# Projecting the values of two strided groups with the keys in partitions, in a decoder layer with dilated attention

## Chip, cores and metric

One Trainium2 chip, one core. The kernel is one program launched once. The metric is the device time of that launch in microseconds (us), the median of several executions.

## What is computed

One decoder layer for 512 tokens of width 1024, in float32: adaLN modulation, a mixture of three causal dilated window attentions, a gated convolutional FFN and a last RMSNorm. The part that matters here is the attention:

```python
DSW_PATTERNS = ((128, 1), (512, 4), (2048, 16))     # window, dilation of the three groups
qkv = (h @ w_in).reshape(B, S, 3, DSW_GROUPS, DSW_HEADS, DSW_HEAD_DIM)
for g, (window, dilation) in enumerate(DSW_PATTERNS):
    o, lse = dilated_window_attention(qkv[:, :, 0, g], qkv[:, :, 1, g], qkv[:, :, 2, g], window, dilation)
...
weights = jax.nn.softmax(jnp.stack(lses, axis=0), axis=0)
o = jnp.sum(weights[..., None] * jnp.stack(outs, axis=0), axis=0)
return o.reshape(B, S, D_MODEL).astype(h.dtype) @ w_out
```

In groups 1 and 2 (dilation 4 and 16) a query attends only to keys whose position has the same remainder, so their tokens are ordered by the remainder modulo 4.

## The kernel before

**Strips.** The 16 heads are worked in 8 pairs. A pair n has nine weight strips of 1024 x 128: values of groups 0, 1, 2 (s = 0, 1, 2), then query and key of each group (s = 3 to 8). A strip's raw weights come by DMA (SP's queue) into one of three buffers `raw`. ScalarE (ACT) writes their high part `wh` (`split_qkv`, profile line L1059), VectorE (DVE) writes the low part `wl` = raw - wh (L1348), each into a slot of a ring of four, of which three are in use after the first pair. TensorE (PE) multiplies a strip in 24 matmuls: for each of the eight tiles of the model width wl x hh, wh x hh, wh x hl (L742, L743, L744). The weights are the stationary operand and the 512 tokens are moving, so the product has the head dimension in partitions and tokens in columns. ACT copies it out of the bank (L1115).

**Values are turned.** The product of probabilities and values (`weigh_values`) wants values with the keys in partitions. So a value strip goes to `v_t`, and `turn_values` transposes it on PE, four blocks of 128 tokens (L784), for groups 1 and 2 each block taking every fourth token. DVE (groups 0 and 2, L1403) or ACT (group 1, L1118) then copies it into `v_n`.

**The order.** `bodies` runs body(n) for n = 0 to 8: pair n is projected while pair n-1 is attended. All engines walk the same 18 half strips h (s = h // 2) and hang their other work on them by hand-written tables. In bodies 1 to 7:

- PE at h: half strip h, then by table a turn of values (`TURN_V_AT`, h = 3, 5, 7), scores (`SCORE_AT`: d = 0, 1 at h = 0, d = 2, 3 at h = 4), transposed probabilities and their product with the values (h = 12 to 16).
- ACT at h: splitting the high part of a strip (`split_at`: at even h, strip h // 2 + 2), at odd h copying out strip s, and exponentials of score part d (`MASK_AT`: d = 0 to 3 at h = 0, 1, 4, 5; L1130).
- DVE at h: the low part of the same strip, a step of the adaLN sum `acc` (L1453, eight to a body; step t = 4, at h = 5, waits for the second half of `ada_raw` to land), copying turned values, and at `MASK_AT` masking the scores and taking their maximum (L1418, ending with `nmax`, L1424), which the exponentials wait for.
- SP: `load_strips` issues strip s once the high and low part of strip s - 3 are made. The second half of `ada_raw` (L529) is issued behind strip 5, once the first four steps of `acc` are done.

PE waits for the low part of a strip at its first half (`l_ready`). ACT waits for the raw weights and for the strip that used the slot before (`strip_done`). Every engine runs its own list in order, so what stands behind a waiting instruction waits too.

Of the kernel before, what the change touches and what calls it, by code (L numbers as in the profile page):

```python
# [26 lines left out]
T = 512  # L27
D = 1024
KT = D // P
# [3 lines left out]
GROUPS = 3  # L33
# [11 lines left out]
RING = 3  # L45
# [35 lines left out]
def decoder_layer(nc, x, c, w_ada, b_ada, norm_mix, norm_ffn, attn_w_in, attn_w_out,  # L81
# [11 lines left out]
    with ctx:  # L93
# [154 lines left out]

        SCORE_AT = {0: (0, 1), 4: (2, 3)}
        MASK_AT = {0: 0, 1: 1, 4: 2, 5: 3}  # L250
        TURN_V_AT = {3: 0, 5: 1, 7: 2}
        ADA_READ_AT = {0: 0, 1: 1, 2: 2, 3: 3, 5: 4, 6: 5, 7: 6, 8: 7}
        ADA_AT = 10
        TURN_P_AT = {12: (0, 1), 14: (2, 3)}
# [33 lines left out]
            return banks[s] if is_first(n) and s in (2, 3) else proj[(par + s) % 2]  # L288

        def qkv_slot(n, s):  # L290
            return RING if is_first(n) and s == RING else s % RING

        def score_bank(d, hd):

# [5 lines left out]

        def split_at(n, h):

            if h % 2:
                return None
            if is_first(n) and h < 8:
                return h // 2 + FIRST if h < 4 else None
            return h // 2 + 2

        def out_slot(o):

# [336 lines left out]
        def _(pe):  # L647
# [91 lines left out]
            def half_strip(bank, slot, half, xh, xl):  # L739
# [4 lines left out]
                    last = nc.tensor.matmul(bank[:], wh[:, slot, t], xl[:, t], start=False, stop=(t == KT - 1))  # L744
                return last

            def make_scores(n, par, d):

                if d == 0:
                    pe.wait_ge(strip_taken, STRIPS * n)  # L750
                if d == 1:
                    pe.wait_ge(ada_taken, n)
                if d >= 2:
                    pe.wait_ge(masked, 4 * (n - 1) + d - 1)
                side, tiles = d // 2, (2 * (d % 2), 2 * (d % 2) + 1)
                for b in tiles:
                    at = HALF * (b % 2)
                    if side == 0:
                        lo = P * max(b - 1, 0)
                        for hd in range(2):  # L760
                            e = slice(E * hd, E * (hd + 1))
                            last = nc.tensor.matmul(score_bank(d, hd)[:, at + (P if b == 0 else 0):at + HALF],  # L762
                                                    q_t[e, par, 0, P * b:P * (b + 1)],
                                                    k_t[e, par, 0, lo:P * (b + 1)], start=True, stop=True)
                    else:
                        for g in (1, 2):
                            for hd in range(2):
                                e = slice(E * hd, E * (hd + 1))
                                last = nc.tensor.matmul(score_bank(d, hd)[:, at + P * (g - 1):at + P * g],  # L769
                                                        q_t[e, par, g, P * b:P * (b + 1)],  # L770
                                                        k_t[e, par, g, P * b:P * (b + 1)], start=True, stop=True)
                last.then_inc(scored, 1)

            def turn_values(n, par, g):
                k, use = g % 2, g // 2
                pe.wait_ge(strip_taken, STRIPS * n + g + 1)
                if use:
                    pe.wait_ge(v_taken[0], 2 * n + 1)
                elif not is_first(n):
                    pe.wait_ge(o_summed, n)  # L780
                src = v_t[:, (par + g) % 2]
                for b in range(NT):
                    keys = src[:, P * b:P * (b + 1)] if g == 0 else src[:, b:T:4]
                    last = nc.tensor.transpose(o_acc[k][:, P * b:P * (b + 1)], keys, ident[:])  # L784
                last.then_inc(v_turned[k], 1)
# [23 lines left out]
            def weigh_values(n, par, j, project):  # L809

                for hd in range(2):
                    pe.wait_ge(p_taken[hd], 4 * (n - 1) + j + 1)
                if j == 0:
                    pe.wait_ge(o_summed, n)
                    if project:
                        pe.wait_ge(v_taken[0], 2 * n + 2)
                        pe.wait_ge(v_taken[1], n + 1)
                side = j // 2
                blocks = p_blocks(j)
                for i, (b, part) in enumerate(blocks):  # L820
                    first = i == 0 or blocks[i - 1][0] != b
                    final = i == len(blocks) - 1 or blocks[i + 1][0] != b
                    for hd in range(2):
                        e = slice(E * hd, E * (hd + 1))
                        if side == 0:
                            values = v_n[:, par, 0, b - 1 + part, e]
                        else:
                            values = v_n[:, par, 1 + part, b, e]
                        last = nc.tensor.matmul(o_acc[side][e, P * b:P * (b + 1)], values,  # L829
                                                p_t[:, (2 * j + hd) % PT_RING, P * i:P * (i + 1)],  # L830
                                                start=first, stop=final)
                last.then_inc(pv_done, 1)
# [37 lines left out]
            def body(n, par, project, attend):  # L870
                filled = 0
                for h in range(2 * FIRST if is_first(n) else 0, HALVES):
                    s = h // 2
                    if project:
                        g = STRIPS * n + s
                        if h % 2 == 0:
                            pe.wait_ge(l_ready, g + 1)
                            pe.wait_ge(strip_taken, s - RING if is_first(n) and s < FIRST + 2 else g - 1)
                        last = half_strip(qkv_bank(n, par, s), qkv_slot(n, s), h % 2, hh, hl)
                        if h % 2 == 1:  # L880
                            last.then_inc(strip_done, 1)
                        turn_v_at = TURN_V_FIRST if is_first(n) else TURN_V_AT
                        if h in turn_v_at:
                            turn_values(n, par, turn_v_at[h])
                        if h == (ADA_FIRST if is_first(n) else ADA_AT):
                            sum_ada(n)
                    if attend:
                        if h in SCORE_AT:
                            for d in SCORE_AT[h]:
                                make_scores(n, 1 - par, d)  # L890
                        for j in PV_AT.get(h, ()):
                            weigh_values(n, 1 - par, j, project)
                        for j in (TURN_P_AT if project else TURN_P_LAST).get(h, ()):
                            for u in (2 * j, 2 * j + 1):
                                turn_probs(n, u, project)
                    if attend and not project and h in FILL_AT:
                        begin_out(fill_steps[filled:filled + FILL_AT[h]])
                        filled += FILL_AT[h]
# [128 lines left out]
        def _(act):  # L1027
# [31 lines left out]
                nc.scalar.activation(dst, src, ACT.Copy).then_inc(done, 1)  # L1059

            def split_qkv(n, s):
                g = STRIPS * n + s
                free = None if isinstance(g, int) and g <= RING else (strip_done, g - RING + 1)
                slot = qkv_slot(n, s)
                split_h(raw_in[s % RING], 16 * (GROUPS * n + s // RING + 1), raw[:, s % RING], wh[:, slot],
                        free, h_ready)

            def copy_rows(c):

# [31 lines left out]
            def body(n, par, project, attend):  # L1101
                for h in range(HALVES):
                    s = h // 2
                    if project:
                        if split_at(n, h) is not None:
                            split_qkv(n, split_at(n, h))
                        if h % 2 == 1:
                            act.wait_ge(strip_done, STRIPS * n + s + 1)
                            kind, g = strip_of(s)

                            if is_first(n) and s == 2:
                                act.wait_ge(v_turned[0], 1)
                            dst = {"v": v_t[:, (par + g) % 2], "q": q_t[:, par, g], "k": k_t[:, par, g]}[kind]
                            src, dst = in_order(g, kind, qkv_bank(n, par, s)[:], dst)
                            nc.scalar.activation(dst, src, ACT.Copy).then_inc(strip_taken, 1)  # L1115
                        if (TURN_V_FIRST if is_first(n) else TURN_V_AT).get(h) == 1:
                            act.wait_ge(v_turned[1], n + 1)
                            nc.scalar.activation(v_n[:, par, 1].rearrange("p b e -> p (b e)"), o_acc[1][:], ACT.Copy  # L1118
                                                 ).then_inc(v_taken[1], 1)
# [174 lines left out]
        def _(dve):  # L1294
# [104 lines left out]
                start_low(c)  # L1399

            def take_values(n, g, dst):
                dve.wait_ge(v_turned[0], 2 * n + g // 2 + 1)
                nc.vector.tensor_copy(dst, o_acc[0][:]).then_inc(v_taken[0], 1)  # L1403

            def take_probs(n, j, project):
# [391 lines left out]
```

## Time and profile before

| | |
|---|---|
| median of 3 runs | 971.48 us (971.14 to 971.8) |
| the profiled execution | 971.24 us |
| its span, first to last instruction | 969.2 us |
| PE busy | 943.0 us, 97% of the span |
| DVE busy | 598.9 us, 62% |
| ACT busy | 447.9 us, 46% |
| TensorE clock granted, mean | 0.996 of full |

The profile is of one execution. Times in it are counted from the start of the span. A matmul's shown duration holds its latency too and overlaps the next one's, so what a matmul costs in a stream is the distance between starts.

### The profile page before, as it was taken

The numbers are of one execution on the slowest core, as the hardware profiler recorded it, in microseconds if no ns is written. First come the engines' busy times: TensorE is split into PE (matmuls) and PEld (weight loads), VectorE is DVE, ScalarE is ACT, GpSimd is POOL, SyncE is SP. The second block draws the span as 40 slices with busy tenths as digits, with TensorE's granted clock in tenths as the row PEclk, the third lists the DMA queues.
The fourth block names the chain that finished last, engine by engine and source line by source line (L and its number), as shares of the span: only waits on it lengthen the run. The fifth ranks groups of instructions, "written<-read, shape, count | busy, mean of one in ns | idle before, by whom it ended". The sixth has DMA issues, their size and how long they took to land.

```text
span 969.2 us, 16362 instructions
## 1 busy us (share of the span) xinstructions
PE 943.0 (97%) x5828; PEld 800.2 (83%) x5828; DVE 598.9 (62%) x1304; ACT 447.9 (46%) x804; POOL 19.9 (2%) x39
## 2 busy tenths in 40 slices
PE   7999999999999999999999899999999999999996
PEld 6687887888888888888787788889999999888884
DVE  3445655725737457366473757899999999633325
ACT  7244434436344354363443455655555556523222
POOL 2000000000000000000000001400000000000000
PEclk9999999999999999999999999999999999999999
DMA  9765342433424323344143022433343343532302
GB/s 310 237 199 149 113 127 65 122 118 108 132 62 130 110 91 102 108 124 136 44 131 108 23 58 74 109 88 87 92 125 87 87 124 93 156 105 87 108 1 87
DMA packets 151538, 107.01 MB, mean 110 GB/s; under 512 B 3510, under 2 KB 138830, under 8 KB 151502
## 3 DMA queue, kind: packets, MB, share of 16 engines
q1 hardware_dynamic: 151296, 106.45, 36.6%
q8 instruction: 23, 0.38, 0.2%
q14 instruction: 13, 0.11, 0.0%
q10 hardware_dynamic: 206, 0.08, 0.0%
HBM read 104.42 MB, written 2.10 MB: 110 GB/s over the span
## 4 chain that ended last, share of the span: by engine, by line
PE 73%; DVE 14%; issue 5%; ACT 5%; POOL 1%; DVEq 1%; ACTq 0%; POOLq 0%
PE bank L742 14%; PE bank L744 13%; PE bank L743 13%; DVE wl L1348 4%; PE bank L1002 4%; PE bank L1001 4%; PE bank L1003 4%; PE bank L829 3%; PE bank L805 3%; DVE gate_in L1619 3%; ACT wh L1059 2%; PE bank L769 1%; DVE sums L1653 1%; DVE sums L1650 1%; PE bank L762 1%
## 5 line engine op out<-in xcount | busy, mean ns | idle before, releaser
L1348 DVE TENSOR_TENSOR wl<-raw,wh 128x1024 fp32r<-128x1024 f32 (+1 forms) x127 | 150.1, 1183 | 175.5 <-ACT wh L1059 174.9
L742 PE MATMUL bank<-hh,wl 128*128 128x512 f32 x544 | 221.3, 407 | 0.0
L744 PE MATMUL bank<-hl,wh 128*128 128x512 f32 x544 | 215.4, 396 | 0.0
L743 PE MATMUL bank<-hh,wh 128*128 128x512 f32 x544 | 215.2, 396 | 0.0
L1059 ACT ACTIVATE wh<-raw 128x1024 fp32r<-128x1024 f32 (+1 forms) x127 | 130.1, 1026 | 63.6 <-PE bank L1003 52.2
L742 PEld LDWEIGHTS bank<-hh,wl 128*128 128x128 f32 x544 | 102.7, 189 | 25.8 <-issue 3.5
L744 PEld LDWEIGHTS bank<-hl,wh 128*128 128x128 f32 x544 | 102.4, 188 | 24.4
L743 PEld LDWEIGHTS bank<-hh,wh 128*128 128x128 f32 x544 | 102.6, 189 | 21.5
L952 PE MATMUL bank<-th,wl 128*128 128x256 f32 x304 | 87.4, 287 | 5.2 <-DVE up_late L1687 4.3
L1130 ACT ACTIVATE probs<-probs,nmax 128x256 f32<-128x256 f32 (+1 forms) x128 | 61.9, 485 | 65.8 <-DVE nmax L1424 65.8
L954 PE MATMUL bank<-th,wh 128*128 128x256 f32 x304 | 85.5, 281 | 0.0
L955 PE MATMUL bank<-tl,wh 128*128 128x256 f32 x304 | 85.5, 281 | 0.0
L952 PEld LDWEIGHTS bank<-th,wl 128*128 128x128 f32 x304 | 57.3, 189 | 8.8 <-DVE up_late L1687 7.6
L952 PE MATMUL bank<-fh,wl 128*128 128x256 f32 x228 | 64.2, 282 | 0.2 <-DVE wl L1348 0.2
L954 PE MATMUL bank<-fh,wh 128*128 128x256 f32 x228 | 64.1, 281 | 0.0
L955 PE MATMUL bank<-fl,wh 128*128 128x256 f32 x228 | 64.1, 281 | 0.0
L1001 PE MATMUL bank<-act_h,wl 128*128 128x512 f32 x160 | 63.4, 396 | 0.0
L1002 PE MATMUL bank<-act_h,wh 128*128 128x512 f32 x160 | 63.4, 396 | 0.0
L1003 PE MATMUL bank<-act_l,wh 128*128 128x512 f32 x160 | 63.4, 396 | 0.0
L954 PEld LDWEIGHTS bank<-th,wh 128*128 128x128 f32 x304 | 57.4, 189 | 0.0
L955 PEld LDWEIGHTS bank<-tl,wh 128*128 128x128 f32 x304 | 57.4, 189 | 0.0
L1059 ACT ACTIVATE wh<-sums 128x1024 fp32r<-128x1024 f32 x38 | 40.5, 1065 | 33.8 <-DVE sums L1653 24.0
(217 smaller groups left out, 1604.2 us busy)
## 6 DMA issues: line engine op xcount, KB each, us to landing
raw<-in_attn_w_in SPq DMA_DIRECT2D x72, 512.0 KB, 3.8
raw<-in_ffn_w_up SPq DMA_DIRECT2D x34, 512.0 KB, 4.0
ada_raw<-in_w_ada SPq DMA_DIRECT2D x16, 1024.0 KB, 5.9
raw<-in_ffn_w_down SPq DMA_DIRECT2D x17, 512.0 KB, 3.3
raw_up<-in_ffn_w_up SPq DMA_DIRECT2D x10, 512.0 KB, 5.1
ada<-in_w_ada SPq DMA_DIRECT2D x16, 256.0 KB, 6.8
raw<-in_attn_w_out SPq DMA_DIRECT2D x8, 512.0 KB, 4.3
raw_up<-in_ffn_w_down SPq DMA_DIRECT2D x5, 512.0 KB, 3.4
```

Source lines behind the costliest of these rows:

```text
L742: nc.tensor.matmul(bank[:], wl[:, slot, t], xh[:, t], start=(t == 0), stop=False)
L743: nc.tensor.matmul(bank[:], wh[:, slot, t], xh[:, t], start=False, stop=False)
L744: last = nc.tensor.matmul(bank[:], wh[:, slot, t], xl[:, t], start=False, stop=(t == KT - 1))
L952: nc.tensor.matmul(bank[:, 0:HALF], low, xh[:, t], start=(fresh and t == 0), stop=False, skip_group_check=True)
L954: nc.tensor.matmul(bank[:, 0:HALF], high, xh[:, t], start=False, stop=False, skip_group_check=True)
L955: last = nc.tensor.matmul(bank[:, 0:HALF], high, xl[:, t], start=False, stop=(final and t == HK - 1), skip_group_check=True)
L1001: nc.tensor.matmul(y[:], wl[:, u, o], act_h[:, u], start=start, stop=False)
L1002: nc.tensor.matmul(y[:], wh[:, u, o], act_h[:, u], start=False, stop=False)
L1003: last = nc.tensor.matmul(y[:], wh[:, u, o], act_l[:, u], start=False, stop=False)
L1059: nc.scalar.activation(dst, src, ACT.Copy).then_inc(done, 1)
L1130: last = nc.scalar.activation(tile, tile, ACT.Exp, bias=nmax[:, side, b, hd:hd + 1], scale=SCORE_SCALE, accum_out=stat[:, side, b, 1, hd:h ...
L1348: nc.vector.tensor_tensor(dst, src, high.bitcast(F32), ALU.subtract).then_inc(done, 1)
```

## The change

Groups 1 and 2 of the values are projected the other way round in bodies 1 to 7. In `key_block` the stationary operand is a block of 128 tokens, every fourth one (`hh[:, t, b:T:4]`), and the moving operand is 256 columns: the weights of group 1 and of group 2 side by side, from slots 1 and 3 of the ring (`wh[:, 1:4:2, t]`). Four such blocks take the place of strips 1 and 2, one at each of h = 2 to 5. Their product has the keys in partitions already and is copied straight into `v_n`. The first pair stays as it was.

Both strips' weights must be there at h = 2, and both slots stay occupied until h = 5 is done. So strip 2 goes to the fourth slot, and strip 4, which uses slot 1, is no longer split at h = 4 but at h = 6, with the wait for strip 2's product (`strip_done` of 9n + 3); strip 5 is split at h = 7 (before: h = 6). Group 0's turn of values is at h = 4 (before: 3); the turns of groups 1 and 2 and their two copies are gone.

```diff
-        TURN_V_AT = {3: 0, 5: 1, 7: 2}
+        TURN_V_AT = {4: 0}
+        KEYS_AT = {2: 0, 3: 1, 4: 2, 5: 3}
...
         def qkv_slot(n, s):
-            return RING if is_first(n) and s == RING else s % RING
+            return RING if s == (RING if is_first(n) else 2) else s % RING
...
         def split_at(n, h):
-            if h % 2:
+            if is_first(n) and h < 8:
+                return h // 2 + FIRST if h in (0, 2) else None
+            if not is_first(n) and h in (4, 6, 7):
+                return {4: None, 6: 4, 7: 5}[h]
+            return None if h % 2 else h // 2 + 2
+
+        def qkv_free(n, s):
+            g = STRIPS * n + s
+            if isinstance(g, int) and g <= RING:
                 return None
-            if is_first(n) and h < 8:
-                return h // 2 + FIRST if h < 4 else None
-            return h // 2 + 2
+            return strip_done, g - 1 if s == 4 and not is_first(n) else g - RING + 1
...
+            def key_block(n, par, b):
+                bank = qkv_bank(n, par, 1 + b // 2)
+                out = bank[:, HALF * (b % 2):HALF * (b % 2 + 1)]
+                for t in range(KT):
+                    keys = slice(b, T, 4)
+                    nc.tensor.matmul(out, hh[:, t, keys], wl[:, 1:4:2, t], start=(t == 0), stop=False)
+                    nc.tensor.matmul(out, hh[:, t, keys], wh[:, 1:4:2, t], start=False, stop=False)
+                    last = nc.tensor.matmul(out, hl[:, t, keys], wh[:, 1:4:2, t], start=False, stop=(t == KT - 1))
+                return last
...
                         if h % 2 == 0:
-                            pe.wait_ge(l_ready, g + 1)
+                            pe.wait_ge(l_ready, g + 2 if s == 1 else g + 1)
...
-                        last = half_strip(qkv_bank(n, par, s), qkv_slot(n, s), h % 2, hh, hl)
+                        if h in KEYS_AT:
+                            last = key_block(n, par, KEYS_AT[h])
+                        else:
+                            last = half_strip(qkv_bank(n, par, s), qkv_slot(n, s), h % 2, hh, hl)
...
+                            if s in (1, 2) and not is_first(n):
+                                src = qkv_bank(n, par, s)[:].rearrange("p (b g e) -> p g b e", b=2, g=2)
+                                dst = v_n[:, par, 1:3, 2 * (s - 1):2 * s]
```

## Rows read from the trace of the kernel before

**Rows 1.** The page: span, and TensorE's line of busy time.
```profile
span 969.2 us, 16362 instructions
PE 943.0 (97%) x5828; PEld 800.2 (83%) x5828; DVE 598.9 (62%) x1304; ACT 447.9 (46%) x804; POOL 19.9 (2%) x39
```
**Rows 2.** Busy time by stretch: bodies 1 and 6, of equal length.
```profile
core 0: us, PE busy (x) PEld busy (x) DVE busy (x) ACT busy (x) POOL busy (x), PEclk, DMA share, GB/s
90.72:154.21 63.49, 63.49 (x372) 51.67 (x372) 35.13 (x101) 27.07 (x58) 0.00 (x0) 1.00 0.36 109
...
408.18:471.67 63.49, 63.49 (x372) 51.68 (x372) 35.74 (x102) 28.00 (x59) 0.00 (x0) 1.00 0.36 108
```
**Rows 3.** Timeline, TensorE with 512 columns: start, duration, engine, line.
```profile
402.32 0.19 PEld L742 LDWEIGHTS bank<-hh,wl 128*128 128x128 f32 x1 [0.17 <-issue]
402.43 0.19 PEld L743 LDWEIGHTS bank<-hh,wh 128*128 128x128 f32 x1
...
403.12 0.39 PE L742 MATMUL bank<-hh,wl 128*128 128x512 f32 x1
...
407.31 0.40 PE L742 MATMUL bank<-hh,wl 128*128 128x512 f32 x1
```
**Rows 4.** Timeline, TensorE with 256 columns, in the FFN.
```profile
699.98 0.29 PE L952 MATMUL bank<-th,wl 128*128 128x256 f32 x1
...
705.66 0.28 PE L952 MATMUL bank<-fh,wl 128*128 128x256 f32 x1
```
**Rows 5.** Timeline around group 1's turn of values in body 6.
```profile
426.30 0.40 PE L744 MATMUL bank<-hl,wh 128*128 128x512 f32 x1
...
426.54 0.63 PE L784 MATMUL bank<-ident,v_t 128*128 128x128 f32 x4
...
427.24 0.40 PE L743 MATMUL bank<-hh,wh 128*128 128x512 f32 x1
```
**Rows 6.** Weight loads: every fourth token (min/median/max ns), and contiguous ones (mean ns).
```profile
L784 PEld LDWEIGHTS bank<-ident,v_t x4: 197/207/212, 426.3 to 426.8; 128*128 128x128 f32 x4
...
L742 PEld LDWEIGHTS bank<-hh,wl 128*128 128x128 f32 x544 | 102.7, 189 | 25.8 <-issue 3.5
...
L792 PEld LDWEIGHTS bank<-ident,acc 128*128 128x128 f32 x32 | 4.0, 141 | 1.1
```
**Rows 7.** Timeline of body 6: strip 2's low part, then the steps to strip 5's.
```profile
409.40 1.23 DVE L1348 TENSOR_TENSOR wl<-raw,wh 128x1024 fp32r<-128x1024 f32 x1
...
420.55 0.37 SPq L529 DMA_DIRECT2D ada_raw<-in_w_ada  x1
...
426.70 0.75 DVE L1453 SCALAR_TENSOR_TENSOR acc<-ada_raw,cond,acc 128x512 f32<-128x512 f32 x1 [2.02 <-DMA ada_raw<-in_w_ada]
...
428.86 0.17 DVE L1424 TENSOR_SCALAR nmax<-stat 128x4 f32<-128x4 f32 x1
...
431.06 1.04 ACT L1059 ACTIVATE wh<-raw 128x1024 fp32r<-128x1024 f32 x1
...
432.13 1.23 DVE L1348 TENSOR_TENSOR wl<-raw,wh 128x1024 fp32r<-128x1024 f32 x1 [3.10 <-ACT wh L1059]
...
433.01 0.48 PE L742 MATMUL bank<-hh,wl 128*128 128x512 f32 x1
```
**Rows 8.** Timelines: strip 5's low part in bodies 1, 3 and 7; a table load.
```profile
114.84 1.23 DVE L1348 TENSOR_TENSOR wl<-raw,wh 128x1024 fp32r<-128x1024 f32 x1 [3.10 <-ACT wh L1059]
...
217.96 1.28 ACT L1059 ACT_TABLE_LOAD   x1
...
242.70 1.23 DVE L1348 TENSOR_TENSOR wl<-raw,wh 128x1024 fp32r<-128x1024 f32 x1 [3.10 <-ACT wh L1059]
...
495.25 1.22 DVE L1348 TENSOR_TENSOR wl<-raw,wh 128x1024 fp32r<-128x1024 f32 x1 [3.10 <-ACT wh L1059]
```
**Rows 9.** Transfers: time to landing of all 16 of `ada_raw`; raw strips issued behind one.
```profile
DMA to landing us min/median/max: 5.4/5.9/7.1
...
421.23 28.10 SPq L522 DMA_DIRECT2D raw<-in_attn_w_in  x6
```

More of the change, by code:

```diff
@@ L777, in turn_values @@
                 if use:
-                    pe.wait_ge(v_taken[0], 2 * n + 1)
+                    pe.wait_ge(v_taken[0], 1)
                 elif not is_first(n):
@@ L815, in weigh_values @@
                     if project:
-                        pe.wait_ge(v_taken[0], 2 * n + 2)
-                        pe.wait_ge(v_taken[1], n + 1)
+                        pe.wait_ge(v_taken[0], n + 2)
+                        pe.wait_ge(v_taken[1], 1)
                 side = j // 2
@@ L1061, in split_qkv @@
             def split_qkv(n, s):
[L1062 to L1066, printed above, removed]
+                split_h(raw_in[s % RING], 16 * (GROUPS * n + s // RING + 1), raw[:, s % RING], wh[:, qkv_slot(n, s)],
+                        qkv_free(n, s), h_ready)
             def copy_rows(c):
@@ L1112, in body @@
                                 act.wait_ge(v_turned[0], 1)
-                            dst = {"v": v_t[:, (par + g) % 2], "q": q_t[:, par, g], "k": k_t[:, par, g]}[kind]
-                            src, dst = in_order(g, kind, qkv_bank(n, par, s)[:], dst)
+                            if s in (1, 2) and not is_first(n):
+                                src = qkv_bank(n, par, s)[:].rearrange("p (b g e) -> p g b e", b=2, g=2)
+                                dst = v_n[:, par, 1:3, 2 * (s - 1):2 * s]
+                            else:
+                                dst = {"v": v_t[:, (par + g) % 2], "q": q_t[:, par, g], "k": k_t[:, par, g]}[kind]
+                                src, dst = in_order(g, kind, qkv_bank(n, par, s)[:], dst)
                             nc.scalar.activation(dst, src, ACT.Copy).then_inc(strip_taken, 1)
@@ L1401, in take_values @@
             def take_values(n, g, dst):
-                dve.wait_ge(v_turned[0], 2 * n + g // 2 + 1)
+                dve.wait_ge(v_turned[0], g // 2 + 1 if is_first(n) else n + 2)
                 nc.vector.tensor_copy(dst, o_acc[0][:]).then_inc(v_taken[0], 1)
```

## The prediction

> **What bounds the kernel now.** First the page: the span is 969.2 us and PE is busy 943.0 of it, 97%, against 62% for DVE and 46% for ACT [rows 1]. A share over the whole says little about one stage, so next the busy time by stretch: each of the full bodies takes 63.49 us, and PE is busy for all 63.49 of them, at the full granted clock (1.00, the 2.4 GHz level) [rows 2]. The reader is to see that no wait of PE is left in the projection loop. Whatever shortens PE's list there shortens the body, until another engine's chain is late. The change can act in seven bodies (1 to 7). I measure places in a body from the edges of those stretches (408.18 for body 6) and call that its phase.
>
> **PE's own work, per body.** Two value strips are 48 matmuls of 512 columns now. Eighteen of them lie between 403.12 and 407.31, so one costs 4.19 / 18 = 0.2328 us [rows 3], and 48 cost 11.17 us. The new blocks are 96 matmuls of 256 columns. The FFN has that form: 48 between 699.98 and 705.66, 5.68 / 48 = 0.1183 us each [rows 4]; 96 cost 11.36 us. That is +0.19 us, the same columns in twice as many instructions.
>
> Removed are two turns, those behind h = 5 and h = 7. Around the first, two matmul starts that in a stream lie 2 x 0.2328 = 0.466 us apart are 427.24 - 426.30 = 0.94 us apart [rows 5]: a turn costs 0.474 us, with its four transposes and the breaks at both ends. The second looks the same. Two give -0.95 us. Group 0's turn only moves from the end of h = 3 to that of h = 4 and costs PE the same; its copy on DVE falls ahead of the mask of d = 2, into time in which DVE waits for scores. The two copies out of the bank that vanish (one ACT, one DVE) gain nothing by themselves, as PE does not wait for either engine now [rows 2]. PE alone: -0.76 us a body, -5.3 us in seven.
>
> **The strided stationary operand.** No row has a float32r load of every fourth column. The nearest are the transposes of v_t, whose loads step by the same four elements: 207 ns against 141 ns for a contiguous transpose load, 66 ns more [rows 6]. A contiguous load of the matmul form shows 189 ns [rows 6], but the next one starts 0.11 us after it [rows 3], so it holds the weight path about 0.11 us and hides under a 0.118 us matmul, barely. From below: the load may hide altogether under the matmul (118 ns). From above: 66 ns are added in full to 110, 176 ns a matmul, 96 x 0.058 = +5.5 us a body. I take 118 to 125 ns, because four strided transposes take 0.63 us [rows 5], so with one latency of about 0.28 us at the end they start some 0.12 us apart, each with its strided load; the excess, at most 0.6 us a body, falls ahead of h = 6 and is swallowed by the wait below.
>
> The Trainium skill speaks against this operand: "SBUF — State Buffer", section "Door 1: The DMA port swizzle", says that SBUF reads run at full rate only with at least two hits in a 16-byte line, and four float32 elements are 16 bytes, so each read here touches a new line. The 207 against 141 ns [rows 6] agree that there is a price. By that rule the matmuls would be load-bound, which is the third case below; by the transposes' spacing they are not.
>
> **Waits that the new order makes.** At h = 2 PE now needs strip 2 as well. Its low part is done at 409.40 + 1.23 = 410.63, phase 2.5 [rows 7]; h = 2 begins near phase 4.4 (after the body's edge PE still has the first scores and one half strip of 12 x 0.2328 = 2.79 us). It is hidden with 2 us to spare.
>
> Strip 4 is the delicate one. It stands at h = 6 in the lists of ACT and DVE, which is behind the exponentials and the mask of d = 3. That is just where strip 5 stands today, so the trace of before shows when it will be ready. In body 6: the ada transfer is issued at 420.55; DVE waits 2.02 us for it and starts step t = 4 at 426.70; then the mask of d = 3, whose maximum comes at 428.86; four exponentials; the split at 431.06; the low part from 432.13 to 433.36, phase 25.18 [rows 7]. None of these steps waits for the slot (PE leaves h = 5 near 426.5) or for what the change takes away. Today strip 5 is needed only at h = 10, so nobody sees this chain. With the change PE wants strip 4 at h = 8.
>
> When does PE reach h = 8? Today at 433.01, phase 24.83 [rows 7]; without the two turns and with the blocks' +0.19 at phase 24.07. The ends of strip 5's low part in the seven bodies are at phases 25.35, 25.51, 26.23, 25.04, 26.50, 25.18 and 24.80 [rows 7, 8]. Bodies 3 and 5 are late because ACT loads a table for 1.28 us at their start [rows 8]. The mean is 25.52. With 0.1 us from semaphore to first matmul the wait is 25.52 + 0.1 - 24.07 = 1.55 us a body, 10.8 us in seven.
>
> One thing may shorten it. The ada transfer takes 5.4 to 7.1 us, median 5.9 [rows 9], and about 6.1 in the seven places that count. Behind it go the raw loads of strips 6 and 7 [rows 9]. Strip 7's buffer will be free only after the new, later split of strip 4, so one competitor of 512 KB is gone. Between no gain and 0.7 us (the fastest of the 16) I take 0.3: an estimate from these rows. The wait becomes 1.25 us a body, 8.7 us in seven.
>
> Behind the waiting matmul stands all of PE's list, and every later anchor moves with it, so nothing is given back. DVE has one more low part and one less copy between h = 6 and h = 8, some 0.5 us later against work at h = 12 and on, where PE also comes 0.5 us later: no second wait. Strips 5 to 8 are loaded and split with several us to spare.
>
> **Sum.** -5.3 + 8.7 = +3.4 us. The profiled execution took 971.24 us (span 969.2) and the median of the runs is 971.48, 0.24 away. I forecast 971.48 + 3.4, about **975 us**. Without the gain in the transfer it would be 977, with the full 0.7 about 972.
>
> **Rivals.**
>
> *Hidden after all (faster).* Strip 4 is ready in time because the ada transfer lands before about 425.5 in body 6 instead of 426.7 and correspondingly elsewhere. Then only PE's own -5.3 us is left: 966 us. For it: a competitor in the queue is removed, and it decides at 1.5 us earlier on average. Against it: no transfer of the 16 was faster than 5.4 us, 0.7 less than the mean here. A mixture, the wait gone in bodies 4, 6 and 7 and halved elsewhere, is a draw.
>
> *A draw.* The transfer gains 0.5 to 1.0 us, or a turn was worth more than 0.47: 970 to 973 us.
>
> *The strided weight load is the bound.* 176 ns a matmul gives -0.95 + 0.19 + 5.5 = +4.7 us a body, and the wait for strip 4 is then covered: +33 us, 1005 us. If a strided load took twice the 0.11 us, 0.22, it would be 96 x 0.102 = +9.8 us, +63 us, 1035. It decides from about 0.131 us a matmul: up to there the excess hides in the wait. For it: the 66 ns. Against it: the transposes' spacing.
>
> *The change does not do what it says* is not to be expected: instructions fall by eight transposes and rise by 48 matmuls a body whatever the time.
>
> **Chances.** The new wait with a loss of over 0.2%: 0.50. Draw, within 0.2% (1.9 us, about what a measurement of this kernel can tell from no change): 0.19. Faster: 0.20. Strided loads bound: 0.11, also slower. Slower in all 0.61. For the range I leave out the strided-load case and a little at each end: 967 to 982 us, where 982 is the 977 of no gain in the transfer plus 0.7 us a body for a slower restart or a chain that slips.
>
> **What the profile after would show.** The chain of waits in the loop: PE at L742 (h = 8) waiting for DVE's L1348, about 1.2 us, seven times, longest in bodies 3 and 5; bodies of about 64.0 us with PE busy some 62.7. The blocks' matmuls 118 to 125 ns apart, their loads above 189 ns. The ada transfer landing in 5.4 to 6.1 us. I am wrong if that wait is missing (transfer early), if the blocks' starts lie over 131 ns apart, or if a wait shows at h = 2 or at the transposes of h = 12.

## The result, and the profile after

The changed kernel takes 1045.43 us (median of 4 runs, 1044.4 to 1049.79), the kernel before 971.31 us beside it: a ratio of 1.0775 (95% interval 1.0741 to 1.0809), 74 us slower. I had forecast 975 us, in a range of 967 to 982. The direction was right, the size wrong by a factor of twenty, and the direction was right by another mechanism than the one I forecast: the case that I had given 11 in 100, the strided load as the bound, is what happened, and in its dearer form.

The page of the changed kernel, with the lines that answer to those of before [rows 1], the new matmul and its weight load, and the queue that fetches instructions:

```profile
span 1044.1 us, 16891 instructions
## 1 busy us (share of the span) xinstructions
PE 1014.1 (97%) x6108; PEld 886.0 (85%) x6108; DVE 595.5 (57%) x1297; ACT 444.5 (43%) x797; POOL 19.9 (2%) x39
...
q8 instruction: 42, 0.69, 0.3%
...
L761 PE MATMUL bank<-wl,hh 128*128 128x256 f32 x224 | 89.1, 398 | 0.0
...
L761 PEld LDWEIGHTS bank<-wl,hh 128*128 128x128 f32 x224 | 73.5, 328 | 1.2
```

PE is as busy as before, 97%. Its share says nothing about the loss; the mean of one load does: 328 ns, where a contiguous load of this form shows 189 [rows 6].

Busy time by stretch, bodies 1 to 3 (same columns as [rows 2]):

```profile
90.67:164.31 73.64, 73.64 (x412) 64.10 (x412) 34.55 (x100) 26.54 (x57) 0.00 (x0) 1.00 0.31 93
164.31:239.76 75.45, 73.89 (x412) 64.02 (x412) 35.93 (x102) 29.27 (x60) 0.00 (x0) 1.00 0.31 92
239.76:313.41 73.65, 73.65 (x413) 64.13 (x412) 34.54 (x100) 27.02 (x57) 0.00 (x0) 1.00 0.31 93
```

A body went from 63.49 us [rows 2] to 73.64, at the same full granted clock of 1.00. Two of the seven (the second here, and body 4) are 1.8 us longer still. The timeline of the changed kernel shows both causes. First the blocks, in body 2: the start of the block at h = 2 (168.86), two matmuls inside it that are 21 apart (170.84 and 175.74), and the last matmul of the block at h = 4 (185.31):

```profile
168.86 0.28 PE L761 MATMUL bank<-wl,hh 128*128 128x256 f32 x1
...
170.84 0.40 PE L761 MATMUL bank<-wl,hh 128*128 128x256 f32 x1
...
172.81 0.33 PEld L761 LDWEIGHTS bank<-wl,hh 128*128 128x128 f32 x1
...
175.74 0.40 PE L761 MATMUL bank<-wl,hh 128*128 128x256 f32 x1
...
185.31 0.40 PE L763 MATMUL bank<-wh,hl 128*128 128x256 f32 x1
...
234.75 0.40 PE L752 MATMUL bank<-hl,wh 128*128 128x512 f32 x1
...
236.71 0.50 PE L750 MATMUL bank<-hh,wl 128*128 128x512 f32 x1 [1.56 <-ACT k_t L1138]
```

4.90 / 21 = 0.2333 us a matmul, twice the 0.1183 of 256 columns in the FFN [rows 4]; over the three blocks in a row, 72 matmuls, 16.45 / 71 = 0.2317. The last two rows stand at the end of body 2 and the start of body 3, where the loop over two bodies jumps back. PE is idle for 1.56 us there. The view names ACT's copy as the releaser, but PE's wait at that point is for an older strip, long copied.

The sum closes with these. The blocks take 96 x 0.2317 = 22.24 us instead of 11.17, which is +11.07. A later kernel with contiguous blocks and no wait for a strip (below, new slots) has bodies of 62.59 us, 0.90 shorter than before, and its blocks take 96 x 0.117 = 11.2 us, 0.03 more than the strips had; so two turns are worth about 0.93 us. That gives +10.14 us a body (measured 10.15), 71.0 in seven; two jumps of 1.84 us add 3.7. Together 74.7 us, against 74.1 between the medians.

### The profile page after: what moved, and what is told of

It is laid out like the page before. It is cut to its first block, busy times and chain, and to the rows that moved or that the text cites. A ratio compares the mean times of both kernels' runs of the same rounds, so it can differ in the third digit from the quotient of the medians.

```text
span 1044.1 us, 16891 instructions
## 1 busy us (share of the span) xinstructions
PE 1014.1 (97%) x6108; PEld 886.0 (85%) x6108; DVE 595.5 (57%) x1297; ACT 444.5 (43%) x797; POOL 19.9 (2%) x39
## 4 chain that ended last, share of the span: by engine, by line
PE 73%; DVE 13%; issue 5%; ACT 5%; POOL 1%; DVEq 1%; DMA 1%; SPq 1%; ACTq 0%
PE bank L750 10%; PE bank L752 10%; PE bank L751 10%; PE bank L761 5%; PE bank L763 5%; PE bank L762 5%; DVE wl L1371 4%; PE bank L1023 4%; PE bank L1025 4%; PE bank L1024 4%; PE bank L848 3%; PE bank L824 3%; DVE gate_in L1642 2%; ACT wh L1081 2%; PE bank L788 1%
## 5 line engine op out<-in xcount | busy, mean ns | idle before, releaser
L750 PE MATMUL bank<-hh,wl 128*128 128x512 f32 x432 | 174.5, 404 | 3.2 <-ACT k_t L1138 3.2
L752 PE MATMUL bank<-hl,wh 128*128 128x512 f32 x432 | 170.9, 396 | 0.0
L751 PE MATMUL bank<-hh,wh 128*128 128x512 f32 x432 | 170.7, 395 | 0.0
L750 PEld LDWEIGHTS bank<-hh,wl 128*128 128x128 f32 x432 | 81.3, 188 | 24.9 <-ACT k_t L1138 4.0
L763 PE MATMUL bank<-wh,hl 128*128 128x256 f32 x224 | 89.1, 398 | 0.0
L761 PE MATMUL bank<-wl,hh 128*128 128x256 f32 x224 | 89.1, 398 | 0.0
L762 PE MATMUL bank<-wh,hh 128*128 128x256 f32 x224 | 89.0, 397 | 0.0
L761 PEld LDWEIGHTS bank<-wl,hh 128*128 128x128 f32 x224 | 73.5, 328 | 1.2
L763 PEld LDWEIGHTS bank<-wh,hl 128*128 128x128 f32 x224 | 73.8, 329 | 0.0
L762 PEld LDWEIGHTS bank<-wh,hh 128*128 128x128 f32 x224 | 73.6, 329 | 0.0
```

What stands on the lines that cost most here:

```text
L750: nc.tensor.matmul(bank[:], wl[:, slot, t], xh[:, t], start=(t == 0), stop=False)
L751: nc.tensor.matmul(bank[:], wh[:, slot, t], xh[:, t], start=False, stop=False)
L761: nc.tensor.matmul(out, hh[:, t, keys], wl[:, 1:4:2, t], start=(t == 0), stop=False)
L762: nc.tensor.matmul(out, hh[:, t, keys], wh[:, 1:4:2, t], start=False, stop=False)
L763: last = nc.tensor.matmul(out, hl[:, t, keys], wh[:, 1:4:2, t], start=False, stop=(t == KT - 1))
```

## Experiments

Each time is a median: of 10 executions for the contiguous, the ordered and the new-slots kernel and the control, 8 for every second token, 4 for the two other versions with TensorE's program written out, and 2 for the rest, whose effects are far above the scatter. Each ratio is to the kernel before, run beside it.

### The pace of the blocks: the step, or the form?

Contiguous tokens, the one edit in `key_block` (the blocks then project other tokens than they should):

```diff
-                    keys = slice(b, T, 4)
+                    keys = slice(P * b, P * (b + 1))
```

> The changed kernel with one edit: each block takes 128 tokens in a row as its stationary operand instead of every fourth one (so it projects other tokens than it should; every count, shape, wait and the moving operand stay). Theory A, the step of four elements in the weight load sets the pace of the blocks (0.233 us a matmul in the changed kernel): here their starts lie 0.118 us apart, the 96 of a body take 11.4 us instead of 22.4, and the time falls by about 7 x 11.0 = 77 us less what then shows of the wait for strip 4 that I had forecast: 972 to 980 us, with TensorE waiting 0.8 to 2.5 us at h = 8 for the low part of strip 4. Rival B, the moving operand in two runs of 128 columns from slots 1 and 3 (or the form as such) sets the pace: 0.233 us stays and the time stays near 1045 us.

Measured: 971.99 us, ratio to the kernel before 1.001 (1.0001 to 1.002). Theory A holds, at the lower edge of its range, and rival B falls: the form and the moving operand in two runs cost nothing. Two rows of this kernel's timeline, 12 matmuls apart, 1.40 / 12 = 0.117 us each; then the row of this line's loads, with their mean:

```profile
164.87 0.28 PE L761 MATMUL bank<-wl,hh 128*128 128x256 f32 x1
...
166.27 0.28 PE L761 MATMUL bank<-wl,hh 128*128 128x256 f32 x1
...
L761 PEld LDWEIGHTS bank<-wl,hh 128*128 128x128 f32 x224 | 42.1, 188 | 1.2
```

Every second token:

```diff
+                    keys = slice(HALF * (b // 2) + b % 2, HALF * (b // 2 + 1), 2)
```

> The changed kernel with every second token as stationary operand (other tokens than it should project; all else stays). A step of two float32 elements still has two reads in each 16-byte line. If the price is one of lines touched once, as the Trainium skill has it, the blocks run at 0.118 us a matmul and the time is that of the contiguous kernel, 972 to 980 us. If any step other than one breaks a doubled read, the pace stays 0.233 us and the time 1045 us.

Measured: 972.91 us, ratio 1.0021 (1.0009 to 1.0033), loads of 196 ns, matmuls 0.120 us apart. A step of two costs nearly nothing. "Any step but one" falls.

Every eighth element, across two tiles (`hh8` and `hl8` are those views):

```diff
+                    hh8 = hh[:, pair].rearrange("p a (j r) -> p (a j) r", r=8)[:, :, b + 4 * (t % 2)]
...
+                    nc.tensor.matmul(out, hh8, wl[:, 1:4:2, t], start=(t == 0), stop=False)
```

> The changed kernel with every eighth element over two tiles of the width as stationary operand (the product is of mixed tiles; all else stays): each read in a line of its own, with a line skipped between. If the price is a fixed one per line, nothing changes against a step of four: 0.233 us a matmul, 1045 us. If it grows with the distance, or skipped lines cost too, the matmuls are slower than 0.233 us and the time above 1060 us. If a line skipped spares a conflict, it is below 1030 us.

Measured: 1051.68 us, ratio 1.0831 (1.0809 to 1.0853), loads of 336 to 339 ns, matmuls 0.242 us apart. So the price is nearly fixed once each read has a line of its own; a skipped line adds 4%. It does not grow with the distance.

Every third token:

```diff
+                    keys = slice(b, b + 3 * P, 3)
```

> The changed kernel with every third token as stationary operand (other tokens than it should project; all else stays). 128 reads with a step of three float32 elements touch 96 lines of 16 bytes, of four 128, of two 64. If the load's time goes with the lines touched, 0.233 us x 96 / 128 = 0.175 us a matmul, 96 x 0.057 x 7 = 38 us above the contiguous edit: about 1010 us. If it is a matter of the step alone being above two, it is 0.233 us and 1045 us; if every step under a line is free, 973 us.

Measured: 1007.93 us, ratio 1.038 (1.0359 to 1.0401). The forecast by lines touched, 1010, was missed by 2 us; the two rivals, 1045 and 973, are out. Its rows (four loads apart are 12 matmuls: 172.87 - 170.75 = 2.12, 0.177 us each) and the mean load:

```profile
170.75 0.27 PEld L761 LDWEIGHTS bank<-wl,hh 128*128 128x128 f32 x1
...
172.87 0.26 PEld L761 LDWEIGHTS bank<-wl,hh 128*128 128x128 f32 x1
...
L761 PEld LDWEIGHTS bank<-wl,hh 128*128 128x128 f32 x224 | 58.8, 262 | 1.2
```

| step, float32 elements | lines of 16 bytes in 128 reads | load shown, ns | us a matmul of 256 columns |
|---|---|---|---|
| 1 | 32 | 188 | 0.117 |
| 2 | 64 | 196 | 0.120 |
| 3 | 96 | 262 | 0.177 |
| 4 | 128 | 328 | 0.233 |
| 8 | 128, every second skipped | 338 | 0.242 |

From 64 lines on, each 32 more add 66 ns to the load shown and 57 ns to the pace: about 1.8 ns a line. At 64 lines and at 32 the pace is nearly the same (0.120 and 0.117), close to half of the 0.2328 us of 512 columns [rows 3], so there the 256 columns set it as far as these rows tell; no run separates them from a contiguous load.

Do load and streaming add up? 512 moving columns under the same strided load (the blocks then compute another product):

```diff
-                out = bank[:, HALF * (b % 2):HALF * (b % 2 + 1)]
+                out = bank[:]
...
-                    nc.tensor.matmul(out, hh[:, t, keys], wh[:, 1:4:2, t], start=False, stop=False)
+                    nc.tensor.matmul(out, hh[:, t, keys], hh[:, t], start=False, stop=False)
```

> The changed kernel with its strided stationary operand, but 512 moving columns (the normalised input's own high and low parts in a row, into the whole bank; so the blocks compute another product) instead of 256. Theory A, the load holds the weight path for 0.233 us whatever streams: 512 columns take 0.233 us themselves in the kernel before, so doubling the columns is free, 0.23 to 0.24 us a matmul and 1043 to 1050 us. Rival B, the streaming of the blocks is what is slow, or load and streaming add up: 0.35 us or more a matmul, 96 x 0.116 x 7 = 78 us more, 1120 us and up.

Measured: 1049.04 us, ratio 1.0804 (1.0769 to 1.0838); the profiled execution's span is 1044.3 against 1044.1. The matmuls stand 0.235 us apart. Twice the columns are free: with 256 or with 512 of them the strided load sets a pace of 0.233 to 0.235 us, and load and streaming do not add up.

### Without the step: is the forecast wait there?

The contiguous kernel is what I had priced, so it tests the rest of the forecast. Its timeline at h = 8 of bodies 2 and 6, and the time to landing of the 13 transfers of `ada_raw` in this stretch:

```profile
178.41 0.50 PE L750 MATMUL bank<-hh,wl 128*128 128x512 f32 x1 [0.60 <-DVE wl L1371]
...
434.66 0.19 PEld L750 LDWEIGHTS bank<-hh,wl 128*128 128x128 f32 x1 [1.12 <-DVE wl L1371]
...
DMA to landing us min/median/max: 5.4/5.6/6.6
```

PE waits for the low part of strip 4 in all seven bodies: the load path stood idle 0.22, 1.04, 0.45, 1.06, 0.64, 1.12 and 0.81 us, 5.3 in all. About 0.2 us of each is not lost: body 1, with 0.22, takes 62.63 us, where a body without this wait takes 62.59 (below). That leaves about 4 us by which the matmuls come later. In the changed kernel itself there is no such wait, since PE reaches h = 8 over 10 us later.

The repair with all results kept: hh and hl are written once in the order of the remainders, and the copies out of the banks put group 0 back in order instead of groups 1 and 2.

```diff
-                    nc.scalar.activation(hh[:, t], xs[:, t], ACT.Identity, bias=mod[:, t:t + 1],
+                    nc.scalar.activation(by_rest(hh[:, t]), by_token(xs[:, t]), ACT.Identity, bias=mod[:, t:t + 1],
...
-                    keys = slice(b, T, 4)
+                    keys = slice(P * b, P * (b + 1))
```

> The changed kernel with the step taken out of the load and all results kept: the normalised input hh and hl is written once at the start with the tokens ordered by their remainder modulo 4, so that the blocks read 128 columns in a row; the copies out of the banks put group 0 back in order instead of groups 1 and 2. Theory A: blocks at 0.118 us a matmul, time as for the contiguous edit, 972 to 982 us, and strip 4's low part the visible wait at h = 8 (0.8 to 2.5 us a body). Rival B (the form is slow, not the step): 1045 us. Third theory C, strip 4's wait is hidden: 966 to 969 us.

Measured: 970.87 us, ratio 0.9998 (0.9988 to 1.0007): no change from the kernel before, 1 us under the range of theory A. The load path waits there in six bodies, 4.3 us in all. Rival B falls again; theory C, no wait, too.

New slots, so that strip 4 need not wait for the blocks:

```diff
-            return RING if s == (RING if is_first(n) else 2) else s % RING
+            if is_first(n):
+                return RING if s == RING else s % RING
+            return (0, 1, RING, 0, 2, 1, 0, RING, 2, 0, 1)[s]
...
-            if not is_first(n) and h in (4, 6, 7):
-                return {4: None, 6: 4, 7: 5}[h]
...
-            return strip_done, g - 1 if s == 4 and not is_first(n) else g - RING + 1
+            return strip_done, g - 2
```

> The ordered kernel with another use of the ring of four slots: strip 4 goes to slot 2, which is free early, strip 5 to slot 1, strip 7 to slot 3 and strip 8 to slot 2, so strips 4 and 5 are split at h = 4 and h = 6 as before the change and nothing is late at h = 8. If the wait for strip 4 is the rest of the loss in the ordered kernel, it vanishes and what stays is TensorE's own gain of 0.76 us a body, 966 us, plus up to 2 x 1.8 us if the loop's backward jump costs TensorE as it did in the changed kernel: 966 to 970 us. If the wait was not the cause, it is the time of the ordered kernel.

Measured: 969.34 us, ratio 0.9975 (0.9966 to 0.9985), faster than the kernel before and than the ordered one. No wait for a weight strip is left in its loop. From the first scores of body 1 to those behind body 7 it takes 438.56 us in its profiled execution, the ordered kernel 441.80: 3.2 us less. The medians are only 1.5 us apart; the profiled execution of the new slots began these scores 1.06 us later, of which more below. Busy time by stretch of this kernel, bodies 1 and 2, and PE's start in body 3:

```profile
93.65:156.24 62.59, 62.59 (x412) 53.02 (x412) 34.54 (x101) 24.75 (x57) 0.00 (x0) 1.00 0.36 110
156.24:220.18 63.94, 62.82 (x413) 52.92 (x412) 36.01 (x102) 26.77 (x59) 0.00 (x0) 1.00 0.36 108
...
217.12 0.49 PE L760 MATMUL bank<-hh,wl 128*128 128x512 f32 x1 [1.12 <-ACT k_t L1148]
```

The body that ends with the jump (body 2) is 1.35 us longer; the other such body, body 4, takes 63.73 us, 1.16 longer than body 3 (62.57).

### The idle time at the backward jump

Forty, then sixteen transposes more a body in the kernel before (each of group 0's made eleven times, as here, or five, with `4+1`):

```diff
-                for b in range(NT):
+                for b in [b for b in range(NT) for _ in range(10+1 if g == 0 and not is_first(n) else 1)]:
```

> The kernel before, with 40 transposes more in each of bodies 1 to 7 (each of the four of group 0's turn of values is made eleven times, into the same place), as many TensorE instructions as the changed kernel has. Asked is why TensorE stood idle 1.56 us at the two backward jumps of the loop of the changed kernel, and not in the kernel before. If the longer loop has to be fetched again at each jump: two idle stretches of about 1.5 us at the jumps and 42 packets of instructions instead of 23; time 971.3 + 7 x 40 x 0.107 = 1001.3, plus 3 to 4 us. If it is something of the blocks themselves, 23 packets and no such stretch: 1001 us.

> The kernel before with 16 transposes more a body. If there is a length up to which the loop is held, between that of the kernel before and 40 more: this tells on which side 16 lies. Held: 971.3 + 7 x 16 x 0.107 = 983.3 us and 23 packets of instructions; fetched again: 3 to 4 us more and about 40 packets.

Measured: 1006.51 us (ratio 1.0364, 1.0343 to 1.0384) and 985.98 us (1.0152, 1.0132 to 1.0173). The instruction queue moved 42 and 41 packets, against 23 in the kernel before. PE stood idle twice at L742 at the jumps, 3.3 and 3.6 us in all. The line of the queue on the page with sixteen more, and its waits:

```profile
q8 instruction: 41, 0.67, 0.3%
...
PE bank L742 <- ACT k_t L1115: 3.6, 2, 1.9
```

So it has nothing to do with the blocks: already sixteen transposes more in a body of 372 matmuls bring both the idle time and the packets, which fit a loop that is fetched again at each jump.

PE's program written out, on top of the new slots:

```diff
-            bodies(pe, body)
+            for n in range(PAIRS + 1):
+                body(n, n % 2, n < PAIRS, n > 0)
```

> The ordered kernel with the new slots, and TensorE's program written out body by body, with no loop (same instructions on TensorE in the same order; the other engines keep their loops). If the idle 1.1 to 1.6 us at each of the two backward jumps is the price of the jump in a loop of this length, both idle stretches vanish and the time falls by 2 to 4 us, from 969.3 to 965.5 to 967.5 us. If it is not the jump, it stays 969.

Measured: 964.66 us, ratio 0.9936 (0.9919 to 0.9952), the fastest version. The written-out program is fetched too (37 packets of instructions), but PE does not stop for it: both idle stretches are gone, and body 2 takes 62.56 us:

```profile
153.51:216.07 62.56, 62.56 (x412) 53.00 (x412) 35.42 (x102) 25.39 (x58) 0.00 (x0) 1.00 0.36 110
```

The control, the kernel before with the same edit:

> The kernel before, untouched but for TensorE's program, which is written out body by body with no loop. In the kernel before TensorE does not stand idle at the backward jumps. If writing the program out only spares that idle time where it exists, this kernel takes what the kernel before takes, 971.4 us. If it helps otherwise too (the last step took 4.7 us off, of which the idle stretches at the jumps show some 2.7 us in the bodies' lengths), it is 1 to 4 us faster.

Measured: 971.75 us, ratio 1.0003 (0.9993 to 1.0012), with 35 packets instead of 23. With every body of PE written out, all engines together need 35; with the loop and sixteen transposes more they took 41, so parts were fetched more than once. Writing out helps only where the jump costs. Of the 4.7 us between the medians of the last two versions the bodies with a jump show 2.5 (1.35 + 1.16). Most of the rest lies ahead of the loop: in the profiled executions the first scores began at 93.65 with the new slots and at 90.91 written out, 2.7 us apart, and the next section shows what goes with that.

### A guess about the start that fell

Against the written-out kernel: DVE writes the scaled input `xs` in the order by remainder, so that ACT's writes of hh and DVE's of hl behind it are in a row again.

```diff
-                    nc.scalar.activation(by_rest(hh[:, t]), by_token(xs[:, t]), ACT.Identity, bias=mod[:, t:t + 1],
+                    nc.scalar.activation(hh[:, t], xs[:, t], ACT.Identity, bias=mod[:, t:t + 1],
...
-                nc.vector.tensor_tensor(xs[:, t], xT[:, t], spread1[:], ALU.mult).then_inc(xs_done, 1)
+                nc.vector.tensor_tensor(by_rest(xs[:, t]), by_token(xT[:, t]), by_token(spread1[:]), ALU.mult).then_inc(xs_done, 1)
```

> The same without a loop on TensorE, with the order by remainder made one step earlier at the start: DVE writes the scaled input xs in that order, and the eight high and eight low parts of hh and hl are then written in a row. In the ordered kernels the first scores began 2 to 3 us later than in the kernel before (93.65 against 90.72), with 1.2 instead of 0.76 us for each ACT write of hh and 1.0 instead of 0.64 for each of hl. If that is the cause, the start comes back by 1 to 2.5 us and the time is 963 to 966 us. If the start's end hangs on something else, it stays that of the kernel without a loop.

Measured: 965.12 us (ratio 0.9935, 0.9916 to 0.9954), the same as without this edit. ACT's writes of hh did fall from 1.30 to 0.81 us and DVE's of hl from 1.09 to 0.69, but DVE's `xs` rose from 0.68 to 1.09, and the first scores began at 91.33. In the written-out kernel, with the strided writes, they had begun at 90.91. So the late starts that I had read in two profiles (92.59 and 93.65) were not made by the strided writes alone; the version with forty transposes, whose start is untouched, began at 92.03 as well.

What the late starts have in common is the granted clock between 25 and 30 us. The row of this stretch for the new slots, then for the written-out kernel:

```profile
25.00:30.00 5.00, 4.42 (x16) 2.40 (x20) 5.00 (x8) 0.00 (x0) 0.00 (x0) 0.66 1.11 331
...
25.00:30.00 5.00, 5.00 (x29) 2.70 (x29) 4.96 (x8) 1.08 (x2) 0.00 (x0) 1.00 1.13 327
```

The clock is 0.66 or 0.67 there, a mixture of its two levels, in four of the fourteen profiled executions: the ordered kernel, the new slots, forty transposes more, and the control. Their first scores began at 91.93 to 93.65; in the ten others, at 1.00, they began at 90.31 to 91.33. The edit does not explain this: the control has the same instructions there as the kernel before. No run tests whether the lower clock alone makes the delay. Without the dip the strided writes cost nothing that shows: 90.91 with them (the written-out kernel), 90.31 to 91.04 in the kernels without. With it, two kernels with strided writes began at 92.59 and 93.65 and two without at 91.93 and 92.03; four executions do not tell whether that gap is theirs.

## Why the prediction was wrong

**The step that failed** is "The strided stationary operand", where I took "118 to 125 ns" a matmul. It was 233. The blocks' starts over 131 ns apart were one of the signs of being wrong that I had named. This term alone is 96 x (0.2317 - 0.1183) x 7 = 76 us. The row used was the strided load of a transpose, 207 ns against 141, four of them 0.12 us apart [rows 5, 6]. Both readings are true of a transpose and do not carry over: in the matmul form the same step of four makes 328 of 188 ns, 140 ns more instead of 66, and a matmul takes 0.233 us instead of 0.117. For the same reason my upper bound, 66 ns added to 110, was no bound. The form twice the 0.11 us, priced at 1035 us, was the right mechanism. It stood in a sentence among the rivals but not in the range. I had also let the transposes' pace outvote the rule of the Trainium skill, "SBUF — State Buffer", section "Door 1: The DMA port swizzle": full rate only with two or more hits in a 16-byte line. The steps of two and three agree with it closely: two elements a line cost next to nothing (972.91 us), and from there the price goes with the lines touched. Measured on the matmul form it was decisive. Why a transpose pays less for the same pattern no run here shows.

**PE's own work** was forecast at -0.76 us a body; with a contiguous load it is -0.90 (62.59 against 63.49). The turns were priced rightly, 0.47 us each; the blocks add 0.03 us instead of 0.19, since they run at 0.117 us a matmul and not at the FFN's 0.1183.

**The wait for strip 4** was the step on which the forecast rested, and its mechanism was right: the contiguous kernel waits at that place, for DVE's low part, in seven bodies. The size was about 4 us of matmul time (5.3 of idle load path) instead of 8.7. In the contiguous kernel the low part ends at phase 24.41 on the average of the seven bodies, 1.10 us ahead of the 25.52 taken from before, where I had allowed 0.3. Two terms make that up. From the issue of the ada transfer to the step t = 4 pass 5.63 us instead of 6.22, 0.6 earlier. And in bodies 3 and 5 the transfer is issued at phases 11.98 and 12.02 instead of 13.80 and 13.79, another 0.5 on the average of seven: PE's idle time at the jump falls just ahead of these two bodies, and presumably it moves their edges against the lists of the other engines; no run tests that. Moving strip 4 to a free slot took the wait away, and the loop became 3.2 us shorter than the ordered kernel's. In the changed kernel the wait is covered, as the third rival had said; so nothing of the 74 us comes from it, though it was my reason for "slower".

**The jump** I had not foreseen: 3.7 of the 74 us. I had counted the instructions ("rise by 48 matmuls a body whatever the time") and given them no price beyond their own duration.

**The draw and the faster rival.** The form that I had priced gives 971.99 us, +0.7, the draw. That it lies inside my range is partly luck: PE gains 0.14 us a body more than I took and the wait is about half as long, and against both stand two jumps at which PE is idle for 3.0 us in all, which had no term. 966 us came within reach only with three further edits: the order at the start, the new slots and the written-out program.

## What to carry to other kernels

Look at the stationary operand's step first when tokens are put in its place. Here steps of one and two cost next to nothing, and steps of three and four were dearer than the 256 columns that ran over them. Order the data once where it is written. A price taken from another mode of the same engine (here a transpose for a matmul) is not a bound; keep the rival in the range until a row of the same form speaks. When slots are held longer, look for a slot that is free before you move a strip to a later time. When a loop grows, look at the instruction queue's packets. And before you explain a difference of 1 or 2 us between two profiles, compare the granted clock of their first stretches.

## What the runs showed that I had not expected

- The load of 128 float32r columns goes by the 16-byte lines that it touches, about 1.8 ns a line above 64 lines; a step of two is nearly free (0.120 us a matmul), a step of eight costs 4% more than one of four.
- The loop over two bodies runs with 23 packets of instructions and no idle time at the jump in the kernel before. With 16 TensorE transposes more a body there are 41 packets, and TensorE idles up to 1.9 us at each of two jumps (1.1 us and more in the other kernels with a longer loop). Written out, the same instructions run without a stop, with 35 or 37 packets.
- Four of the fourteen profiled executions, the untouched start among them, had a granted clock of 0.66 or 0.67 between 25 and 30 us and came to the loop 1 to 3 us later.
